# Expert weights through ten places instead of eight, gate/up weights in 32 KB rows

## The chip, the cores and the metric

One core of one Trainium2 chip runs the kernel. The metric is the device time of one execution in microseconds. All data is float32.

## What is computed

A decoder layer: a projection, two token mixers side by side, a merge and an output projection, and then a mixture of experts, which is most of the work. 256 tokens and 16 meta tokens go in, each of width 1024. What matters here is the last part:

```python
logits = (tokens @ w_router + b_router).astype(f32)
top_logits, top_idx = lax.top_k(logits, TOP_K)          # 4 of 32 experts
top_w = jax.nn.softmax(top_logits, axis=-1)
...
gu = xb @ w_gate_up[e] + b_gate_up[e]                    # 1024 -> 2048
gate = jnp.minimum(gu[:, ::2], SWIGLU_LIMIT)
up = jnp.clip(gu[:, 1::2], -SWIGLU_LIMIT, SWIGLU_LIMIT)
glu = gate * jax.nn.sigmoid(gate * SWIGLU_ALPHA)
return ((up + 1.0) * glu) @ w_down[e] + b_down[e]        # 1024 -> 1024
```

An expert has 8 MB of gate/up weights and 4 MB of down weights, 32 experts have 384 MB, and every expert is chosen by some token, so all of it is read from HBM once.

## The kernel before

The program is written by hand for each engine; semaphores order the engines. Up to about 260 us it computes the mixers, the merge and the output projection, then the router, then which tokens go to which expert (a chain of small instructions on DVE and PE). After that runs the loop over items. An item is one expert with up to 64 of its tokens; here there are 32 items.

**Pieces and places.** The weights of an item come in six pieces of 2 MB, 16 KB in each of 128 partitions: pieces 0 to 3 are gate/up, 4 and 5 are down. Counted through the whole loop, piece `r` lies in place `r % PLACES` of `ring`; there are eight places, and `HOME` says which stretch of `ring` a place is. `load_piece` (the DMA is issued at line 286) loads one, and the place has a semaphore `landed`. PE adds one to `piece_used` when its last matmul of a piece is done.

**The order of the loads.** All weight loads are issued by SP. Before the loop SP loads pieces 0 to 4 while the mixers end (it waits for `o_mm`, `og_used` and `br_mm` in turn, since the places held other tensors), then the router weights and the small bias rows, and pieces 5 to 7 when the output projection is done (`wo_mm`). From piece 8 on, `load_round` waits for `piece_used` to reach r - 7, that is, until the piece that held the place is consumed. The loop covers `ROUND` = 4 items, 24 pieces or three trips through the places.

**One item on PE** (`item`): four bias matmuls of 32 rows (`ohb` times `bgu`), then for each gate/up piece a wait for `landed` and eight matmuls (two records each in the trace), then `add_last` (the item before is added into x's sum in PSUM) and `gather` (the tokens of the next item), transposes of the activated hidden values and of the gathered tokens, and the two down pieces, eight matmuls each. DVE and ACT do the activation between them.

**The routing on DVE.** Just ahead of the loop DVE builds `oh`, a one-hot table of the experts of the items, and a second copy of it in partitions 32 to 63 (`oh_up`), from which `expert_of` makes the operand `ohb` of the bias matmuls. The bias rows `bgu` lie in 64 partitions, 2048 elements each.

Of the kernel before, what the change touches and what calls it, by code (L numbers as in the profile page):

```python
# [20 lines left out]
P = 128  # L21
META, SEQ = 16, 256
TOK = META + SEQ
D = 1024
# [10 lines left out]
EXTRA = 16  # L35
# [4 lines left out]
PLACES = 8  # L40
ROUND = 4
HOME = [2, 4, 5, 7, 3, 6, 0, 1]
# [41 lines left out]
def build(nc, a, out):  # L84
    with ExitStack() as ctx:
# [15 lines left out]
        grow = sb("grow", [4, 2 * P])  # L101
# [19 lines left out]
        ringf = ring[:, :, :].rearrange("p a b -> p (a b)")  # L121
# [74 lines left out]
        x2 = at(w_mix, 0, TT, D)  # L196
        sumT = at(w_mix, 2048, KD, SEQ)
        xgT = at(w_mix, 4096, 2, 2, 2, SLOTS)
        xgS = at(w_mix, 8576, 512)
        squares = at(w_mix, 2048, D)  # L200
        hT = at(w_mix, 4608, 4, 2, SLOTS)
        gt = at(w_mix, 5120, 512)
        sgm = at(w_mix, 5632, 512)
        up = at(w_mix, 6144, 512)
        ysl = at(w_mix, 6656, 512)
        ctr = at(w_mix, 7168, SEQ)
        pick = at(w_mix, 7424, TT, SLOTS)
        pickw = at(w_mix, 7552, TT, 2, SLOTS)
        ohb = w_mix[0:2 * E, 7808:7808 + SLOTS]
        wrt = at(w_mix, 9472, KD, E)  # L210
        brt = w_mix[:, 9728:9728 + E]
        lgq = at(w_mix, 9760, TT, P)

        gain1, gain2, gain_x = pcol[:, 0:8], pcol[:, 8:16], pcol[:, 32:40]

        gatesf = gates[:, :, :].rearrange("p a b -> p (a b)")
        bgu = gatesf[0:2 * E, 0:2 * D]
        fgain = gatesf[:, 3 * D:4 * D]
# [12 lines left out]
        oh_up = rout[E:2 * E, 480:480 + ITEMS + 2]  # L231
        oh_both = rout[0:2 * E, 480:480 + ITEMS + 2]
        ohc = rout[0:E, 530:530 + EXTRA]
        j3 = rout[0:E, 578:626]
        half = rout[0:1, 626:628]
# [3 lines left out]
        iwt = at(rout, 1256, TT, ITEMS + 2)  # L239
# [4 lines left out]
        for n in """consts xload0 xload1 meta rows ident_in gain1_in gain1_turned gain1_ready s5rows bload cload glu_w branch5_w branchh_w out_w expert_rows  # L244
# [4 lines left out]
                    proj proj_free bu bu_free ph rounded sines scanned xs5 ysum  # L249
                    gelu_in gelu_sig g5_ready glu_mm glu_sig f_sig q_sig og_sig f_ready logf  # L250
# [7 lines left out]
                    ct_mm ct_ready ysl_ready comb0 comb1 added0 added1 piece_used w_last xgs_ready xg_turned  # L258
# [8 lines left out]
        gu_d = a["w_gate_up"].rearrange("l e (i p j) n -> p (l e i) (j n)", i=UP, p=P)  # L267
# [14 lines left out]
        def load_piece(q, e, r):  # L282

            i, place = r % PIECES, r % PLACES
            src = gu_d[:, bass.ds(e * UP + i, 1), :] if i < UP else dn_d[:, bass.ds(e * DOWN + (i - UP), 1), :]
            q.dma_start(ring[:, HOME[place]:HOME[place] + 1, :], src).then_inc(landed[place], 16)

# [4 lines left out]
        def _(sp):  # L292
# [46 lines left out]
            more_rounds = sp.value_load(idx[0:1, ITEMS + 3:ITEMS + 4], min_val=E // ROUND - 1, max_val=ITEMS // ROUND - 1)  # L339

            def load_round(q, last):

                e = None
                for r in range(PLACES, ROUND * PIECES + (0 if last else PLACES)):
# [5 lines left out]
            with sp.Fori(0, more_rounds) as q:  # L350
                load_round(q, False)
            load_round(more_rounds, True)
# [7 lines left out]
        def _(pool):  # L360
# [6 lines left out]
            pool.dma_start(grow[:, :], a["norm2_gain"].rearrange("l (i c) -> (l i) c", c=2 * P)).then_inc(s["grow_in"], 16)  # L367
# [216 lines left out]
        def _(pe):  # L584
# [92 lines left out]
            for j in range(2):  # L677
                last = tr(ps[6][:, 32 + 4 * j:36 + 4 * j], grow[:, :].rearrange("p (c j) -> p j c", j=2)[:, j, :], 4)
# [203 lines left out]
            def turn_gathered(w, bank):  # L882

                pe.wait_ge(s["xgs_ready"], w + 1)
                for b in range(2):
                    for j in range(2):
                        part = xgS[:, 256 * b:256 * (b + 1)].rearrange("p (c j) -> p j c", j=2)[:, j, :]
                        last = tr(ps[bank][:, (2 * b + j) * P:(2 * b + j + 1) * P], part)
                last.then_inc(s["xg_turned"], 1)
# [31 lines left out]
            pe.wait_ge(s["expert_rows"], 32)  # L921
# [572 lines left out]
```

## Time and profile before

| what | value |
|---|---|
| median of 3 runs | 1208.69 us (1208.61 to 1208.96) |
| the profiled execution, its own time | 1208.81 us |
| its span, first to last instruction | 1207.0 us |
| PE busy | 1163.8 us (96% of the span) |
| DVE busy | 442.1 us (37%) |
| ACT busy | 181.5 us (15%) |
| read from HBM | 434.53 MB |
| weight loads gate/up, down | 128 and 64, of 2048 KB each |

The profiled execution's own time is 1.8 us more than its span (what lies around the instructions), and 0.12 us above the median. "PE busy" counts matmuls in flight; "PEld" is the load of the stationary operand into PE. A releaser behind an arrow is what ended a wait. In the time of the loop PE is busy nearly all the time by its records, and so are the DMA engines.

### The profile page before, as it was taken

To read this page: it belongs to the slowest core of one execution; us is meant where nothing else is said; L and a number is where in the kernel's file an instruction comes from. 1 tells how busy PE (TensorE), PEld (TensorE's weight loads), DVE (VectorE), ACT (ScalarE), POOL (GpSimd) and SP (SyncE) were. 2 spreads that over 40 slices of the span, in tenths; PEclk is the share of its full clock that TensorE was granted. 3 is DMA by queue.
4 is the path that set the end of the run, shared out by engine and by line. 5 is a ranking of instruction groups with operands and counts; after the bars stand their busy time and mean duration, and the time that the engine had idled before them with its cause. 6 is when DMAs were issued, how large, how long until landed. Compare 5 with 4: busy or idle time off the path is not lost.

```text
span 1207.0 us, 14299 instructions
## 1 busy us (share of the span) xinstructions
PE 1163.8 (96%) x5532; PEld 501.3 (42%) x5532; DVE 442.1 (37%) x1108; ACT 181.5 (15%) x330; POOL 3.6 (0%) x11
## 2 busy tenths in 40 slices
PE   8999999999999999999999999999999999999996
PEld 7757798763333333333333333333333333333332
DVE  6889883242322222222333222222222222222224
ACT  4435632020000000000000000000000000000002
POOL 1000000000000000000000000000000000000000
PEclk9999998998999999999999999999999999999999
DMA  6444304836999999999999999999999999999994
GB/s 214 175 173 179 137 1 189 342 153 282 426 430 426 429 430 427 428 431 427 428 429 428 428 428 429 427 430 428 428 430 428 427 430 428 428 430 428 428 429 179
DMA packets 47528, 435.91 MB, mean 361 GB/s; under 512 B 10044, under 2 KB 10240, under 8 KB 22864
## 3 DMA queue, kind: packets, MB, share of 16 engines
q1 hardware_dynamic: 46912, 434.93, 86.2%
q10 hardware_dynamic: 400, 0.58, 0.1%
q8 instruction: 15, 0.25, 0.1%
q0 software_dynamic: 192, 0.08, 0.0%
q14 instruction: 9, 0.07, 0.0%
HBM read 434.53 MB, written 1.05 MB: 361 GB/s over the span
## 4 chain that ended last, share of the span: by engine, by line
PE 68%; DMA 26%; DVE 3%; ACT 1%; issue 1%; ACTq 0%; SPq 0%; DVEq 0%
PE ps L586 65%; DMA ring<-in_w_gate_up 25%; PE ps L589 4%; DVE ring L989 1%; ACT ring L382 1%; DMA ring<-in_s_lambda_im 0%; ACT L382 0%; DVE ring L992 0%; DVE ring L1162 0%; DVE ring L995 0%; DVE w_mix L995 0%; DVE rout L992 0%; DVE rout L995 0%; ACT small L382 0%; DVE x L989 0%
## 5 line engine op out<-in xcount | busy, mean ns | idle before, releaser
L586 PE MATMUL ps<-ring,w_mix 128*64 128x512 f32 (+1 forms) x3168 | 710.2, 591 | 23.1 <-DMA ring<-in_w_gate_up 21.8
L586 PEld LDWEIGHTS ps<-ring,w_mix 128*64 128x64 f32 (+1 forms) x3168 | 227.6, 139 | 458.4 <-issue 399.8
L992 DVE TENSOR_SCALAR w_mix<-ps 128x256 f32<-128x256 f32 x128 | 45.3, 416 | 613.2 <-PE ps L586 613.2
L586 PE MATMUL ps<-ring 128*128 128x256 f32 (+7 forms) x920 | 195.7, 397 | 2.7 <-DVE ring L989 2.2
L586 PEld LDWEIGHTS ps<-ring 128*128 128x128 f32 (+2 forms) x920 | 144.0, 187 | 51.1 <-issue 30.0
L586 PE MATMUL ps<-w_mix 64*128 64x512 f32 (+3 forms) x624 | 142.5, 569 | 0.7 <-issue 0.7
L382 ACT ACTIVATE w_mix<-ps 128x512 f32<-128x512 f32 (+1 forms) x104 | 55.0, 529 | 396.3 <-PE ps L589 212.4
L382 ACT ACTIVATE w_mix<-w_mix 128x512 f32<-128x512 f32 x32 | 20.1, 630 | 514.7 <-DVE w_mix L992 514.7
L989 DVE TENSOR_TENSOR x<-ps,x 128x512 f32<-128x512 f32 x136 | 84.3, 679 | 18.1 <-PE ps L586 18.1
L586 PEld LDWEIGHTS ps<-w_mix 64*128 64x128 f32 (+3 forms) x624 | 51.7, 161 | 88.2 <-issue 86.3
L989 DVE TENSOR_TENSOR ring<-ring 128x256 f32<-128x256 f32 (+5 forms) x182 | 76.4, 472 | 6.6 <-PE ps L586 3.7
L589 PEld LDWEIGHTS ps<-cst,w_mix 128*128 128x128 f32 x328 | 43.1, 194 | 58.8 <-issue 26.0
L589 PE MATMUL ps<-cst,w_mix 128*128 128x128 f32 x328 | 63.4, 307 | 0.6
L992 DVE TENSOR_SCALAR w_mix<-cst,rout 128x64 f32<-128x64 f32 x194 | 44.5, 285 | 0.5 <-issue 0.5
L1447 DVE COPY w_mix<-ps 128x512 f32<-128x512 f32 x32 | 22.1, 691 | 50.8 <-PE ps L589 50.8
L586 PE MATMUL ps<-gates,w_mix 32*64 32x512 f32 x256 | 35.7, 627 | 0.6 <-DVE w_mix L989 0.6
L382 ACT ACTIVATE ring<-ring 128x272 f32<-128x272 f32 (+5 forms) x50 | 29.9, 602 | 9.6 <-DVE ring L989 6.6
L989 DVE TENSOR_TENSOR ring<-ps,ring 128x272 f32<-128x272 f32 x64 | 23.6, 427 | 4.0 <-PE ps L586 3.8
L989 DVE TENSOR_TENSOR w_mix<-ps,pcol 128x512 f32<-128x512 f32 x33 | 22.5, 682 | 0.2 <-PE ps L589 0.2
L989 DVE TENSOR_TENSOR w_mix<-w_mix 128x512 f32<-128x512 f32 x32 | 22.1, 692 | 1.1
L995 DVE SCALAR_TENSOR_TENSOR w_mix<-w_mix 128x512 f32<-128x512 f32 x32 | 22.1, 691 | 1.1
L382 ACT ACT_TABLE_LOAD x15 | 19.2, 1283 | 7.1 <-issue 3.6
(145 smaller groups left out, 241.7 us busy)
## 6 DMA issues: line engine op xcount, KB each, us to landing
ring<-in_w_gate_up SPq DMA_DIRECT2D x128, 2048.0 KB, 31.2
ring<-in_w_down SPq DMA_DIRECT2D x64, 2048.0 KB, 35.2
ring<-in_w_in SPq DMA_DIRECT2D x9, 2048.0 KB, 7.9
ring<-in_w_out SPq DMA_DIRECT2D x1, 4096.0 KB, 12.9
w_mix<-in_w_branch_s SPq DMA_DIRECT2D x1, 2048.0 KB, 13.6
w_mix<-in_w_branch_hgrn SPq DMA_DIRECT2D x1, 2048.0 KB, 12.6
x<-in_x SPq DMA_DIRECT2D x2, 512.0 KB, 4.4
w_mix<-in_s_w_glu SPq DMA_DIRECT2D x1, 1024.0 KB, 10.1
```

Of the source, the lines that this page charges most:

```text
L382: return nc.scalar.activation(o, i, fn, **k)
L586: return nc.tensor.matmul(o, l, r, start=start, stop=stop, skip_group_check=True)
L589: return nc.tensor.transpose(o, i, ident[0:n, 0:n])
L989: return V.tensor_tensor(out=o, in0=i0, in1=i1, op=op)
L992: return V.tensor_scalar(o, i, s1, s2, op0, op1) if op1 is not None else V.tensor_scalar(o, i, s1, None, op0)
L995: return V.scalar_tensor_tensor(out=o, in0=i0, scalar=sc, in1=i1, op0=op0, op1=op1)
L1447: V.tensor_copy(hT, ps[3][:, :].rearrange("p (a b c) -> p a b c", a=4, b=2)).then_inc(s["hT_ready"], 1)
```

## The change

It has three parts.

1. **Ten places.** `gates` and `w_mix` become one tensor `mixed` of 14336 elements per partition; when the mixers are done, its upper 8192 hold two more places (`home` gives a place's address). What lay there in the loop moves to the lower part of `mixed` and into a stretch of `cst` that is no longer needed. `bgu` is spread over 128 partitions of 512 elements: `oh_up` gets three copies instead of one, and the four bias matmuls use rows 0-31, 32-63, 64-95 and 96-127. The final gain `fgain` is loaded behind the last weights instead of ahead of the loop. The items before the loop (`HEAD` = 2) are written out, and the loop covers 5 items, 30 pieces, three trips through ten places; the number of items is padded to 2 + 5k, which for 32 is again 32.
2. **The loads ahead of the loop.** All of pieces 0 to 9 are loaded before the first `piece_used`; piece 7 goes where piece 3 went in the order, pieces 3 and 4 go where piece 4 went, piece 5 behind the bias rows, and 6, 8 and 9 behind `wo_mm`.
3. **Pairs.** Each partition of a 4 MB half of the gate/up weights now holds 32 KB that are contiguous in HBM. From piece 12 on, pieces 0 and 1 of an item, and 2 and 3, are loaded by one DMA of 4 MB (`load_pair`) into two places side by side. It waits until both places are free, and PE waits for it at the first of the two pieces. Down pieces are loaded singly, as before. Since `w_gate_up`'s rows are dealt out otherwise, the gathered tokens are transposed with another stride (`turn_gathered`, and `grow`, `gain_x` for the same order).

```diff
-PLACES = 8
-ROUND = 4
-HOME = [2, 4, 5, 7, 3, 6, 0, 1]
+PLACES = 10
+HEAD, ROUND = 2, 5
+HOME = [4, 5, 2, 3, 8, 9, 6, 7, 0, 1]
+RING = 8
...
+        def load_pair(q, e, r):
+
+            i, place = r % PIECES, r % PLACES
+            q.dma_start(home(place, 2).rearrange("p (a n) -> p a n", a=1), gu2_d[:, bass.ds(e * (UP // 2) + i // 2, 1), :])\
+                .then_inc(landed[place], 16)
+
+        def in_pair(r):
+            return r >= PLACES and r % PIECES < UP
...
-            for r in range(3):
+            for r in (0, 1, 2):
                 load_piece(sp, 0, r)
             sp.wait_ge(s["og_used"], 1)
-            load_piece(sp, 0, 3)
+            load_piece(sp, 1, 7)
             sp.wait_ge(s["inv_mm"], 1)
             sp.wait_ge(s["br_mm"], 8)
-            load_piece(sp, 0, 4)
+            for r in (3, 4):
+                load_piece(sp, 0, r)
...
-            sp.wait_ge(s["mrg_ready"], 4)
-            for g in range(2):
-                sp.dma_start(bgu[E * g:E * (g + 1), :], a["b_gate_up"].rearrange("l e n -> (l e) n")).then_inc(s["expert_rows"], 16)
-            sp.dma_start(fgain, a["final_norm_gain"].rearrange("(o n) -> o n", o=1).to_broadcast([P, D])).then_inc(s["lastgain"], 16)
...
+            load_piece(sp, 0, 5)
...
             sp.wait_ge(s["wo_mm"], 4)
-            for r in range(5, PLACES):
-                load_piece(sp, r // PIECES, r)
+            for r in (6, 8, 9):
+                load_piece(sp, 1, r)
...
-                    sp.wait_ge(s["piece_used"], q * (ROUND * PIECES) + (r - PLACES + 1))
-                    load_piece(sp, e, r)
...
+                    if not in_pair(r):
+                        sp.wait_ge(s["piece_used"], q * (ROUND * PIECES) + (r - PLACES + 1))
+                        load_piece(sp, e, r)
+                    elif r % 2 == 0:
+                        sp.wait_ge(s["piece_used"], q * (ROUND * PIECES) + (r - PLACES + 2))
+                        load_pair(sp, e, r)
...
                 def place(i):
                     r = m * PIECES + i
-                    pe.wait_ge(landed[r % PLACES], quad * (ROUND * PIECES // PLACES * 16) + 16 * (r // PLACES + 1))
-                    return ring[:, HOME[r % PLACES], :]
+                    if not (in_pair(r) and r % 2):
+                        first, more = landings(r)
+                        pe.wait_ge(landed[r % PLACES], 16 * first if q is None else q * (16 * more) + 16 * first)
+                    return home(r % PLACES)
...
-            V.tensor_copy(oh_up[:, 0:E], ident[E:2 * E, E:2 * E])
-            V.memset(oh_up[:, ITEMS:ITEMS + 2], 0.0)
+            for g in range(1, 4):
+                V.tensor_copy(oh_up[g - 1][:, 0:E], ident[E * g:E * (g + 1), E * g:E * (g + 1)])
+                V.memset(oh_up[g - 1][:, ITEMS:ITEMS + 2], 0.0)
```

SP's queue ahead of the loop, from the end of the mixers (`o_mm`) to the last load that waits for `wo_mm`. Before:

```order
L286 DMA ring<-in_w_gate_up 128x4096 [waits o_mm]
L286 DMA ring<-in_w_gate_up 128x4096 x2
L286 DMA ring<-in_w_gate_up 128x4096 [waits og_used]
L286 DMA ring<-in_w_down 128x4096 [waits br_mm,inv_mm]
L324 DMA w_mix<-in_w_router 128x8x32 [waits br_mm]
L325 DMA w_mix<-in_b_router 128x32
L329 DMA gates<-in_b_gate_up 32x2048 [waits mrg_ready]
L329 DMA gates<-in_b_gate_up 32x2048
L330 DMA gates<-in_final_norm_gain 128x1024
L333 DMA w_mix<-in_b_down 32x512 [waits ysl_ready]
L286 DMA ring<-in_w_down 128x4096 [waits wo_mm]
L286 DMA ring<-in_w_gate_up 128x4096 x2
```

and now:

```order
L295 DMA ring<-in_w_gate_up 128x4096 [waits o_mm]
L295 DMA ring<-in_w_gate_up 128x4096 x2
L295 DMA ring<-in_w_gate_up 128x4096 [waits og_used]
L295 DMA ring<-in_w_gate_up 128x4096 [waits br_mm,inv_mm]
L298 DMA mixed<-in_w_down 128x4096
L354 DMA mixed<-in_w_router 128x8x32 [waits br_mm]
L355 DMA mixed<-in_b_router 128x32
L358 DMA mixed<-in_b_gate_up 32x512 x4
L298 DMA mixed<-in_w_down 128x4096
L364 DMA mixed<-in_b_down 32x512 [waits ysl_ready]
L295 DMA ring<-in_w_gate_up 128x4096 [waits wo_mm]
L295 DMA ring<-in_w_gate_up 128x4096 x2
```

Seven pieces instead of five are now issued ahead of the wait for `wo_mm`, one of them directly ahead of the router weights.

SP's loop, one item of it (ISA rows are the waits on `piece_used`). Before:

```order
L286 ISA [waits piece_used]
L286 DMA ring<-in_w_down 128x4096
L347 REGISTER_ALU
L286 ISA [waits piece_used]
L286 DMA ring<-in_w_down 128x4096
L346 ISA
L346 TENSOR_LOAD idx
L346 ISA x2
L347 REGISTER_ALU
L286 ISA [waits piece_used]
L286 DMA ring<-in_w_gate_up 128x4096
L347 REGISTER_ALU
```

and now:

```order
L298 ISA [waits piece_used]
L298 DMA ring<-in_w_down 128x4096
L377 ISA
L377 TENSOR_LOAD idx
L377 ISA x2
L382 REGISTER_ALU
L304 ISA [waits piece_used]
L304 DMA ring<-in_w_gate_up 128x8192
L382 REGISTER_ALU
L304 ISA [waits piece_used]
L304 DMA mixed<-in_w_gate_up 128x8192
L379 REGISTER_ALU
```

An item has four loads now where it had six; the two of gate/up weights have 8192 elements per partition.

DVE in the routing, from the copies of the one-hot table to the operands of the last matmuls. Before:

```order
L1374 COPY rout<-cst 32x32
L1375 COPY rout<-cst 32x32
L1376 MEMSET rout 32x2
L1377 CAST idx<-cst 1x32
```

and now:

```order
L1411 COPY rout<-cst 32x32
L1413 COPY rout<-cst 32x32
L1414 MEMSET rout 32x2
L1413 COPY rout<-cst 32x32
L1414 MEMSET rout 32x2
L1413 COPY rout<-cst 32x32
L1414 MEMSET rout 32x2
L1415 CAST idx<-cst 1x32
```

Two copies and two memsets come in here; a little further on a copy of 32x16 (L1395) becomes three of 32x20 (L1433), and one of three small writes of `idx` goes.

## Rows read from the trace of the kernel before

**Rows 1.** The page: bytes moved in 40 equal slices of the span (GB/s)
```profile
GB/s 214 175 173 179 137 1 189 342 153 282 426 430 426 429 430 427 428 431 427 428 429 428 428 428 429 427 430 428 428 430 428 427 430 428 428 430 428 428 429 179
```
**Rows 2.** Windows: start:end and length, busy by engine, PEclk, DMA share, GB/s
```profile
400.00:600.00 200.00, 199.57 (x938) 67.08 (x936) 54.59 (x134) 15.46 (x28) 0.00 (x0) 1.00 1.01 428
700.00:1100.00 400.00, 381.88 (x1769) 124.64 (x1766) 104.43 (x254) 29.93 (x54) 0.00 (x0) 1.00 1.01 429
```
**Rows 3.** The chain that ended last, in time: start, length, what
```profile
609.16 22.27 PE ps L586 x104
...
636.92 22.27 PE ps L586 x104
...
676.48 33.24 DMA ring<-in_w_gate_up
709.76 7.44 PE ps L586 x32
...
734.50 33.95 DMA ring<-in_w_gate_up
...
1145.60 33.96 DMA ring<-in_w_gate_up
1179.60 7.44 PE ps L586 x32
```
**Rows 4.** Timeline of PE, last two items: start, length, what, [idle before <-releaser]
```profile
1150.24 3.65 PE L586 MATMUL ps<-ring,w_mix 128*64 128x512 f32 x16 [1.24 <-DMA ring<-in_w_gate_up]
...
1166.76 1.09 PE L586 MATMUL ps<-gates,w_mix 32*64 32x512 f32 x8
1167.77 10.58 PE L586 MATMUL ps<-ring,w_mix 128*64 128x512 f32 x48
1179.60 3.65 PE L586 MATMUL ps<-ring,w_mix 128*64 128x512 f32 x16 [1.25 <-DMA ring<-in_w_gate_up]
1183.19 3.85 PE L586 MATMUL ps<-w_mix 64*128 64x512 f32 x16
```
**Rows 5.** Windows around the start of the loop (columns as in rows 2)
```profile
270.00:274.00 4.00, 2.73 (x19) 1.24 (x16) 3.12 (x22) 0.60 (x1) 0.00 (x0) 1.00 1.00 430
278.00:284.00 6.00, 6.00 (x22) 1.81 (x20) 0.00 (x0) 0.00 (x0) 0.00 (x0) 0.62 0.00 0
284.00:286.00 2.00, 2.00 (x13) 0.56 (x9) 0.00 (x0) 0.00 (x0) 0.00 (x0) 1.00 0.70 131
286.00:288.00 2.00, 2.00 (x12) 0.70 (x10) 0.00 (x0) 0.00 (x0) 0.00 (x0) 1.00 0.73 287
```
**Rows 6.** Timeline of SP, loads of the places that come free first
```profile
284.24 3.74 SPq L286 DMA_DIRECT2D ring<-in_w_gate_up  x2
294.51 0.33 SPq L286 DMA_DIRECT2D ring<-in_w_down  x1
307.40 0.34 SPq L286 DMA_DIRECT2D ring<-in_w_gate_up  x1
312.37 0.33 SPq L286 DMA_DIRECT2D ring<-in_w_gate_up  x1
```
**Rows 7.** Timeline of DVE in the routing
```profile
269.95 0.17 DVE L1375 COPY rout<-cst 32x32 f32<-32x32 f32 x1
270.07 0.06 DVE L1376 MEMSET rout<- 32x2 f32 x1
270.14 0.17 DVE L1377 CAST idx<-cst 1x32 int32<-1x32 f32 x1
```
**Rows 8.** Windows in which all the data moved in rows of 2 KB, 2 KB, 4 KB, 4 KB
```profile
70.00:73.00 3.00, 3.00 (x8) 1.33 (x7) 3.00 (x9) 0.00 (x0) 0.00 (x0) 1.00 1.05 404
89.00:92.00 3.00, 3.00 (x12) 1.66 (x11) 2.77 (x8) 2.11 (x6) 0.00 (x0) 1.00 1.05 409
76.00:79.00 3.00, 3.00 (x8) 1.33 (x7) 0.00 (x0) 2.60 (x6) 0.00 (x0) 1.00 1.03 412
94.00:97.00 3.00, 3.00 (x29) 1.60 (x28) 3.00 (x8) 1.39 (x4) 0.00 (x0) 1.00 1.02 408
```
**Rows 9.** The loads of line 286, from issue to landing
```profile
DMA to landing us min/median/max: 7.7/31.3/35.3
```
**Rows 10.** Timeline about the router weights: SP, then DVE and PE
```profile
230.72 0.38 SPq L324 DMA_DIRECT2D w_mix<-in_w_router  x1
...
236.27 0.42 DVE L989 TENSOR_TENSOR w_mix<-w_mix,pcol 128x256 f32<-128x256 f32 x1 [3.24 <-DMA w_mix<-in_w_router]
...
244.26 0.60 PE L589 MATMUL ps<-cst,x 128*128 128x128 f32 x4
```

More of the change, by code:

```diff
@@ L230, in build @@
         oh = rout[0:E, 480:480 + ITEMS + 2]
[L231 to L235, printed above, removed]
+        oh_up = [rout[E * g:E * (g + 1), 480:480 + ITEMS + 2] for g in range(1, 4)]
+        oh_all = rout[:, 480:480 + ITEMS + 2]
+        ohc = rout[0:E, 534:534 + EXTRA]
+        j3 = rout[0:E, 576:576 + 3 * EXTRA]
+        half = rout[0:1, 636:638]
         slT = rout[0:E, 640:640 + SEQ]
@@ L257, in build @@
                     pick_ready gathered xg_ready gate_in gate_sg h_done
[L258 removed]
+                    ct_mm ct_ready ysl_ready comb0 comb1 added1 piece_used w_last xgs_ready xg_turned
                     grow_in down_bias last_sum
@@ L284, in load_piece, with landings @@
             i, place = r % PIECES, r % PLACES
-            src = gu_d[:, bass.ds(e * UP + i, 1), :] if i < UP else dn_d[:, bass.ds(e * DOWN + (i - UP), 1), :]
-            q.dma_start(ring[:, HOME[place]:HOME[place] + 1, :], src).then_inc(landed[place], 16)
+            if i < UP:
+                q.dma_start(home(place).rearrange("p (a n) -> p a n", a=1), gu_d[:, bass.ds(e * (UP // 2) + i // 2, 1), i % 2, :])\
+                    .then_inc(landed[place], 16)
+            else:
+                q.dma_start(home(place).rearrange("p (a n) -> p a n", a=1), dn_d[:, bass.ds(e * DOWN + (i - UP), 1), :])\
+                    .then_inc(landed[place], 16)
+        def load_pair(q, e, r):
+            i, place = r % PIECES, r % PLACES
+            q.dma_start(home(place, 2).rearrange("p (a n) -> p a n", a=1), gu2_d[:, bass.ds(e * (UP // 2) + i // 2, 1), :])\
+                .then_inc(landed[place], 16)
+        def in_pair(r):
+            return r >= PLACES and r % PIECES < UP
+        def landings(r):
+            alone = [n for n in range(r % PLACES, r + 1, PLACES) if not (in_pair(n) and n % 2)]
+            per_round = [n for n in range(PLACES, PLACES + ROUND * PIECES)
+                         if n % PLACES == r % PLACES and not (in_pair(n) and n % 2)]
+            return len(alone), len(per_round)
         block = ctx.enter_context(nc.Block())
@@ L676, in _ @@
             tr(ps[6][:, 8:32], prow[:, :], 24)
-            for j in range(2):
-                last = tr(ps[6][:, 32 + 4 * j:36 + 4 * j], grow[:, :].rearrange("p (c j) -> p j c", j=2)[:, j, :], 4)
+            for j in range(4):
+                last = tr(ps[6][:, 32 + 2 * j:34 + 2 * j], grow[:, :].rearrange("p (c j) -> p j c", j=4)[:, j, :], 2)
             last.then_inc(s["rows_turned"], 1)
@@ L884, in turn_gathered @@
                 pe.wait_ge(s["xgs_ready"], w + 1)
[L885 to L888, printed above, removed]
+                for j in range(4):
+                    last = tr(ps[bank][:, j * P:(j + 1) * P], xgS.rearrange("p (c j) -> p j c", j=4)[:, j, :])
                 last.then_inc(s["xg_turned"], 1)
@@ L938, in item @@
                 for b in range(2):
-                    rows = slice(E * b, E * (b + 1))
                     for h in range(2):
-                        last = mm(ps[b][SLOTS * h:SLOTS * (h + 1), :], ohb[rows, :],
-                                  bgu[rows, D * h + 512 * b:D * h + 512 * b + 512], True, False)
+                        rows = slice(E * (2 * b + h), E * (2 * b + h + 1))
+                        last = mm(ps[b][SLOTS * h:SLOTS * (h + 1), :], ohb[rows, :], bgu[rows, :], True, False)
                 last.then_inc(s["ohb_used"], 1)
@@ L968, in item @@
                     if i == 0:
-                        turn_last(pe.snap(w + 2))
-            with pe.Fori(0, n_rounds) as quad:
-                for m in range(ROUND):
-                    item(quad, m)
-            add_last(n_rounds * ROUND)
+                        turn_last(on(w + 2))
+            for m in range(HEAD):
+                item(m)
+            with pe.Fori(0, n_rounds) as q:
+                for m in range(HEAD, HEAD + ROUND):
+                    item(m, q)
+            add_last(n_rounds * ROUND + HEAD)
         @block.vector
@@ L1383, in _ @@
             V.tensor_copy(first, ps[2][0:E, 1:2])
[L1384 removed]
+            link(ts(half[:, 0:1], ps[2][0:1, 2:3], 1.0 / ROUND, 0.4, MU, AD))
             link(ts(half[:, 0:1], half[:, 0:1], MAGIC, None, AD))
             link(ts(half[:, 0:1], half[:, 0:1], MAGIC, None, SU))
[L1387 to L1388 removed]
+            ts(idx[0:1, ITEMS + 2:ITEMS + 3], half[:, 0:1], float((E - HEAD) // ROUND), None, AD)
             ts(idx[0:1, ITEMS:ITEMS + 1], half[:, 0:1], float(ROUND), float(E), MU, AD).then_inc(s["count_ready"], 1)
[L1390 removed]
+            js, ja, jb = (j3[:, EXTRA * k:EXTRA * (k + 1)] for k in range(3))
             link(ts(js, iota_e[0:E, 0:EXTRA], first, None, SU))
@@ L1394, in _ @@
             link(tt(oh[:, E:ITEMS], ja, jb, MU))
-            V.tensor_copy(oh_up[:, E:ITEMS], oh[:, E:ITEMS])
+            for g in range(1, 4):
+                V.tensor_copy(oh_up[g - 1][:, E:ITEMS], oh[:, E:ITEMS])
             link(ts(js, js, 1.0, None, AD))
```

110 lines of the change are left out of this document (59 added, 51 removed).

## The prediction, made before the changed kernel ran

> **What bounds the kernel now.** I began with the page's row of bytes moved [rows 1]. From slice 11 of 40 to the last but one it stands at 426 to 431 GB/s and never gives way, whatever PE is doing: the loop streams weights at one rate. The windows confirm it: 428 and 429 GB/s with a DMA share of 1.01 over 200 and 400 us [rows 2]. Next the chain of waits [rows 3]. Up to about 676 us one item follows another on PE in 27.76 us (609.16 to 636.92) and the chain never leaves PE. From 676 us on it goes in hops of two items through a weight load, the wait of PE ending at 709.76, then 16 items later at 1179.60: 29.37 us per item, 4.894 us per piece of 2 MB, which is 2.097 MB at 428.5 GB/s. So PE would need 27.76 us for an item and DMA needs 29.37. PE lives off the pieces loaded ahead for some 14 items and waits for weights in each item after that. The end of the kernel is therefore **the end of the weight stream, plus what PE does after it**; PE's 96% is no bound by itself, and time saved on PE inside the loop is worth nothing.
>
> Where PE waits: 48 records after the bias matmuls, three pieces of 16, so at piece 3 of an item [rows 4]. The last such wait ends at 1179.60, and what follows (piece 3, `add_last`, both down pieces, the last sum, the norm, the store) is the tail, which nothing shortens.
>
> The other end of the stream: eight pieces are there when the loop begins, and nothing moves between 278 and 284 us [rows 5]; then the first consumed place is loaded, issued at 284.24 [rows 6]. Counting bytes from the right edge of the window that ends at 288, (131 + 287) x 2 = 836 KB or 1.95 us of data: the data begins 2.0 us after the issue. From there 182 pieces (8 to 189) go past until the wait at 1179.60 ends; 182 x 4.894 = 890.7, and the rest, 4.7 us, is start, landing and small gaps.
>
> **The change, term by term.**
>
> *Two pieces more before the stream, -9.8.* Ten instead of eight are loaded before the first `piece_used`, in time when the engines idle. The stream to the last wait is 180 pieces instead of 182: 2 x 4.894. The pieces that move forward need cover. Piece 4 now goes out directly behind piece 3 and ahead of the router weights, and delays them by 4.9 us. They landed at 236.23 and DVE waited for them; with 4.9 more, 0.42 for the product with the gain and 0.69 for the first addition to `x` it is 242.3, and PE wants that addition at 244.26 [rows 10]. Covered, with 2.0 us to spare; without this cover each us would be one on the path. The bias rows and piece 5 land some 5 to 10 us later than the rows they replace did and are not wanted before the loop, 30 us later. `fgain` is issued behind the last weights in a queue that is then full; it lands some 3 us after them and is wanted after the last sum, over 10 us later. Nothing.
>
> *The routing, +0.6.* DVE gets two copies and two memsets of `oh_up`. A copy and its memset take 0.19 us of its time (269.95 to 270.14) [rows 7], so 0.38; two more narrow copies are bounded by 0 and 0.17 each, I take 0.15; one write of `idx`, some 0.09, goes. This chain leads to the first item, so the first consumed piece is 0.6 us later, and the stream with it.
>
> *Gaps in the young stream, +3.6.* Until the places run short, a load is issued when PE has consumed enough, and PE has a rhythm: the fourth piece is consumed at 294.51, the sixth at 307.40, the seventh some 0.4 before 312.37 [rows 6]. Before, each load waits for one piece and the queue stays just filled. Now pieces 12 and 13 wait for the fourth, 14 and 15 for the sixth. With 0.6 for the routing and 2.0 from issue to data: pieces 10 and 11 run from 286.8 to 296.6; the first pair begins at 297.1 (gap 0.5) and ends at 306.9; the second begins at 310.0 (gap 3.1) and ends at 319.8. Pieces 16 and on are issued well before that, and since PE gains 1.6 us on the stream with each item no later pair finds the queue empty. In the steady state at most three places hold pieces not yet consumed, so seven are on order, 34 us of data; the loads of before stand 31.3 us in the queue [rows 9].
>
> *Rows of 32 KB, -4.4.* 60 pairs replace 120 loads. Each engine moves 8 rows a load, so 480 rows per engine go away. The price of a row isn't shown at this size. Rates by row length: 404 and 409 GB/s at 2 KB, 412 and 408 at 4 KB [rows 8], 428.5 at 16 KB. A 2 MB load at 406, 410 and 428.5 takes 5.165, 5.115 and 4.894 us, and has 64, 32 and 8 rows per engine: (5.165 - 4.894) / 56 = 4.8 ns a row, (5.115 - 4.894) / 24 = 9.2 ns. By the one 480 rows are 2.3 us, by the other 4.4. The step from 4 to 16 KB is nearest to the one made here, and I take 4.4. The lower bound is no gain at all, or a loss (below).
>
> The Trainium skill (DMA: Bandwidth & Descriptors, Why small descriptors are slow) gives a fixed overhead of about 3 cycles per packet, at the fabric clock that it names an estimate of 3.5 ns, 1.7 us for 480 rows. By that the sum would be -3.7 us. The trace shows more for a row than this: 4.8 and 9.2 ns.
>
> *The tail, +3.6.* PE now waits for the pair ahead of piece 2, while the bytes of piece 3 arrive when they did. After the last wait PE has one gate/up piece more to do: 3.59 us (1179.60 to 1183.19) [rows 4]. The two down pieces land 10 us later and are wanted later still.
>
> *At nothing:* the bias matmuls keep their number and size, and four row groups take the place of two; if they ran one after the other it would cost an item 1 us at most [rows 4], and 27.76 + 1 is still below 29.2 us. The other stride of the transposes, the registers of the loop and the new addresses are PE, DVE and SP time inside the loop, under the same cover.
>
> Sum: -9.8 + 0.6 + 3.6 - 4.4 + 3.6 = **-6.4 us**. The profiled execution took 1208.81 us, 0.12 above the median; from the median it is 1202.3. The cover is thinner afterwards: an item of the stream takes 29.2 us, PE's 27.76.
>
> **Rivals.**
>
> *The long rows bring nothing* (the engines still move 16 KB at a time, or the cost goes by bytes). For it: between 2 and 4 KB the rate hardly rises [rows 8]. Against: it does rise to 16 KB. Then the sum is -2.0: 1206.7, within the noise.
>
> *The long rows read more slowly.* No row of before is longer than 16 KB; in a pair each engine walks 32 KB at one stretch and the engines start twice as far apart in HBM. The mechanism would sit in the 60 pair loads alone, visible as a lower GB/s in steady windows. Its bound is the rate at 4 KB rows, 410: 120 x 0.221 = 26.5 us, so 1233. It turns the sign from 2.0 + 2.4 = 4.4 us on, spread over 587 us of pairs: 0.75%, a rate of the pairs below 425. Against: the rate rose with every step in row length so far. At 1.5% it is 1206.7 + 8.8 = 1215.5.
>
> *The stream gets fast enough for PE's pace.* If each load carried a fixed price of its own, halving the gate/up loads would give much. Then PE's own rhythm is the end: the fourth piece of item 0 is consumed at 294.51, that of item 31, 31 x 27.76 later, at 1155.1, where it was 1183.2. With 0.6 for the routing that is 27.5 us less, 1181.2. The Trainium skill (SBUF — State Buffer, The DMA setup-cost knee) has such a rule: a fixed 2 us per transfer, so join them; 60 fewer transfers would be 120 us. Against it stands that a 2 MB load takes 4.894 us, less than bytes at 428.5 GB/s plus anything fixed: queued loads overlap. A half-way case is likelier: rows worth twice my price and no gap at the second pair, 1202.3 - 4.4 - 3.6, some 1195 to 1198.
>
> **How the numbers follow.** Forecast with its own spread (row price 2.3 to 4.4, gaps 2 to 5 us, 1200 to 1205.5): 0.60. Long rows bring nothing: 0.15. Slower rows: 0.13, mostly 1209 to 1220. Still faster: 0.12, nearly all above 1195. The range 1197 to 1208 holds the forecast, the case without a gain and half of the faster one. A measurement of this kernel tells 0.2% (2.4 us) from no change: faster is 0.60 + 0.12, same is the 0.15, slower 0.13.
>
> **What would show it.** GB/s in the steady windows at 430 to 431 with an item of 29.2 us; at 428 the rows bring nothing, below 427 they cost. 60 gate/up loads of 4096 KB and 62 single ones behind the ten first. An idle stretch of the engines between 306 and 310 us. PE's waits ahead of piece 2, and 31 us from the end of the last wait to the end of the span, where it was 27.4. The prediction is wrong if PE never waits for weights, if the stream has later gaps, or if the first item starts more than 1 us later.

## The result, and the profile after

The changed kernel takes **1202.76 us** (median of five runs, 1201.16 to 1204.25), beside 1208.69 us for the kernel before (1208.34 to 1210.34 in the same rounds). The ratio is 0.9949, 95% interval 0.9934 to 0.9963: 5.9 us less. The profiled execution has a span of 1200.9 us, where it was 1207.0. The forecast was 1202.3.

The page's row of bytes moved, after (it answers to [rows 1]):

```profile
GB/s 215 175 167 185 140 1 172 405 208 256 391 434 427 429 433 428 429 433 430 429 433 430 429 433 430 429 433 430 429 433 429 430 433 426 432 429 429 431 431 141
```

From slice 12 on the level is 426 to 434, a step above the 426 to 431 of before. The slice ahead of it, with 391, is the gap that the prediction described. The windows show both (columns as in [rows 2]); the first three answer to [rows 5], the last two to [rows 2]:

```profile
278.00:284.00 6.00, 6.00 (x22) 1.55 (x16) 0.00 (x0) 0.00 (x0) 0.00 (x0) 0.54 0.00 0
284.00:286.00 2.00, 2.00 (x12) 0.57 (x10) 0.00 (x0) 0.00 (x0) 0.00 (x0) 1.00 0.00 0
286.00:288.00 2.00, 2.00 (x12) 0.70 (x10) 0.00 (x0) 0.00 (x0) 0.00 (x0) 1.00 0.96 254
305.00:308.00 3.00, 3.00 (x20) 0.76 (x16) 0.00 (x0) 0.00 (x0) 0.00 (x0) 1.00 0.59 251
308.00:310.00 2.00, 2.00 (x16) 0.62 (x16) 0.00 (x0) 0.60 (x1) 0.00 (x0) 1.00 0.91 262
310.00:312.00 2.00, 2.00 (x12) 0.62 (x10) 0.00 (x0) 0.00 (x0) 0.00 (x0) 1.00 0.69 279
400.00:600.00 200.00, 199.69 (x938) 67.22 (x936) 54.62 (x133) 15.45 (x28) 0.00 (x0) 1.00 1.01 431
700.00:1100.00 400.00, 385.28 (x1794) 128.04 (x1792) 109.24 (x266) 30.31 (x55) 0.00 (x0) 1.00 1.00 431
```

SP's timeline after, the loads of the places that come free first (it answers to [rows 6]):

```profile
285.10 3.76 SPq L298 DMA_DIRECT2D ring<-in_w_down  x2
295.38 0.34 SPq L304 DMA_DIRECT2D ring<-in_w_gate_up  x1
308.24 0.33 SPq L304 DMA_DIRECT2D mixed<-in_w_gate_up  x1
312.83 3.79 SPq L298 DMA_DIRECT2D ring<-in_w_down  x2
```

Pieces 10 and 11 at 285.10, the first pair at 295.38, the second only at 308.24. The chain that ended last (it answers to [rows 3]) leaves PE after 16 items and then goes through a weight load every second item:

```profile
724.76 36.22 DMA mixed<-in_w_gate_up
761.02 10.87 PE ps L623 x48
...
1111.60 10.87 PE ps L623 x48
1131.73 38.25 DMA ring<-in_w_gate_up
1170.03 10.87 PE ps L623 x48
```

14 items lie between 761.02 and 1170.03: 29.215 us an item, 4.869 a piece, where it was 4.894. PE's timeline in the last item (it answers to [rows 4]):

```profile
1160.70 1.09 PE L623 MATMUL ps<-mixed,cst 32*64 32x512 f32 x8
1161.72 7.09 PE L623 MATMUL ps<-ring,mixed 128*64 128x512 f32 x32
1170.03 7.09 PE L623 MATMUL ps<-ring,mixed 128*64 128x512 f32 x32 [1.22 <-DMA ring<-in_w_gate_up]
1177.04 3.85 PE L623 MATMUL ps<-mixed,cst 64*128 64x512 f32 x16
```

PE waits after 32 records, at piece 2, and has 32 ahead of it instead of 16. From 1170.03 to the end of the span it is 30.9 us, where it was 27.4. And the page's DMA issues (KB each, median us to landing):

```profile
ring<-in_w_gate_up SPq DMA_DIRECT2D x48, 4096.0 KB, 37.7
ring<-in_w_down SPq DMA_DIRECT2D x50, 2048.0 KB, 35.8
mixed<-in_w_gate_up SPq DMA_DIRECT2D x12, 4096.0 KB, 35.6
mixed<-in_w_down SPq DMA_DIRECT2D x14, 2048.0 KB, 34.3
...
ring<-in_w_gate_up SPq DMA_DIRECT2D x8, 2048.0 KB, 17.1
```

60 gate/up loads of 4 MB; of 64 down loads two are ahead of the loop.

Both kernels, and every experiment, can be cut at the same two points: the first load of the loop, and the end of PE's last wait for weights.

| kernel | first load | to the last wait's end | from there to the end of the span | first load to end |
|---|---|---|---|---|
| before | 284.24 | 895.36 | 27.4 | 922.8 |
| after | 285.10 | 884.93 | 30.9 | 915.8 |
| after, profiled again (experiment 12) | 284.42 | 884.13 | 30.9 | 915.0 |
| after, with idle matmuls ahead of the loop (experiment 8) | 283.28 | 885.37 | 30.9 | 916.2 |

The last three rows issue the same loads from the first one on, so they show how far such a cut scatters by itself: 1.2 us. One profile against another tells differences above that, and no smaller ones.

### The profile page after: what moved, and what is told of

Read it like the earlier page. It is cut to its first block, busy times and chain, and to the rows that moved or that the text cites. A ratio compares the mean times of both kernels' runs of the same rounds, so it can differ in the third digit from the quotient of the medians.

```text
span 1200.9 us, 14064 instructions
## 1 busy us (share of the span) xinstructions
PE 1162.0 (97%) x5534; PEld 503.8 (42%) x5534; DVE 442.9 (37%) x1112; ACT 181.5 (15%) x330; POOL 3.6 (0%) x11
## 4 chain that ended last, share of the span: by engine, by line
PE 68%; DMA 26%; DVE 3%; ACT 1%; issue 1%; ACTq 0%; SPq 0%; DVEq 0%
PE ps L623 64%; DMA ring<-in_w_gate_up 19%; DMA mixed<-in_w_gate_up 6%; PE ps L626 4%; DVE ring L1028 1%; ACT ring L419 1%; DMA ring<-in_s_lambda_im 0%; ACT L419 0%; DVE ring L1031 0%; DVE ring L1199 0%; DVE ring L1034 0%; DVE mixed L1034 0%; DVE rout L1031 0%; DVE rout L1034 0%; ACT mixed L419 0%
## 5 line engine op out<-in xcount | busy, mean ns | idle before, releaser
L623 PE MATMUL ps<-ring,mixed 128*64 128x512 f32 (+1 forms) x2560 | 572.5, 590 | 15.7 <-DMA ring<-in_w_gate_up 14.8
L623 PEld LDWEIGHTS ps<-ring,mixed 128*64 128x64 f32 (+1 forms) x2560 | 187.8, 139 | 362.9 <-issue 330.9
L1031 DVE TENSOR_SCALAR mixed<-ps 128x256 f32<-128x256 f32 x128 | 45.4, 418 | 606.0 <-PE ps L623 606.0
L623 PE MATMUL ps<-mixed,cst 64*128 64x512 f32 (+2 forms) x784 | 163.0, 616 | 1.3 <-issue 0.7
L623 PE MATMUL ps<-mixed 128*64 128x512 f32 (+2 forms) x704 | 151.3, 562 | 3.0 <-DMA mixed<-in_w_gate_up 2.9
L623 PEld LDWEIGHTS ps<-mixed,cst 64*128 64x128 f32 (+2 forms) x784 | 45.5, 151 | 112.1 <-issue 111.3
L623 PEld LDWEIGHTS ps<-mixed 128*64 128x64 f32 (+2 forms) x704 | 54.5, 140 | 88.7 <-issue 79.9
L419 ACT ACTIVATE mixed<-ps 128x512 f32<-128x512 f32 (+1 forms) x87 | 48.4, 557 | 276.3 <-PE ps L623 223.9
L626 PE MATMUL ps<-cst,mixed 128*128 128x128 f32 x262 | 49.4, 310 | 0.6
L1031 DVE TENSOR_SCALAR cst<-cst,rout 128x64 f32<-128x64 f32 x194 | 44.8, 288 | 0.5 <-issue 0.5
```

What stands on the lines that cost most here:

```text
L419: return nc.scalar.activation(o, i, fn, **k)
L623: return nc.tensor.matmul(o, l, r, start=start, stop=stop, skip_group_check=True)
L626: return nc.tensor.transpose(o, i, ident[0:n, 0:n])
L1031: return V.tensor_scalar(o, i, s1, s2, op0, op1) if op1 is not None else V.tensor_scalar(o, i, s1, None, op0)
```

## The experiments

The prediction came true as a sum of terms of both signs. Such a sum can be right by terms that are wrong together, so each was taken apart. Unless said otherwise an edit is one of the changed kernel; times are medians, and ratios are to the kernel before, timed on the same chip in the same rounds (1208.71, 1208.98 and 1208.67 us in the three sets of four). The changed kernel itself was timed again in the third set only (experiment 12).

### 1. No pairs

```diff
         def in_pair(r):
-            return r >= PLACES and r % PIECES < UP
+            return False
```

> Ten places, but every gate/up load single, 2 MB in rows of 16 KB. The sum: 120 loads regain their 480 longer rows per engine (+4.5), the gaps of the young stream close (-3.9) and the last wait is at piece 3 again (-3.4): 1200.0, so faster than the changed kernel. Item of the stream 29.4 us, last wait to end 27.4 us, GB/s 428. Rival, the pairs are what gained and the gaps and the tail cost nothing: 1207 or more.

Measured: **1200.09 us** (1197.75 to 1201.4), 0.9933 [0.9920, 0.9947]. The profile is of the fastest of its runs; the cut takes out what of that lies ahead of the first load. First load to the last wait's end 885.14 us, to the end of the span 912.6: 3.2 less than with pairs. Steady windows:

```profile
400.00:600.00 200.00, 199.69 (x938) 67.32 (x936) 55.73 (x137) 15.77 (x29) 0.00 (x0) 1.00 1.01 428
700.00:1100.00 400.00, 389.39 (x1814) 128.55 (x1812) 109.25 (x266) 30.91 (x56) 0.00 (x0) 1.00 1.01 428
```

The rate is back at 428 and the gap and the long tail (27.4 us) are gone. So the third part of the change, taken alone, costs some 3 us; what it gains by the rate (4.5) is less than what it gives back at the start (3.9) and at the end (3.5).

### 2. Only pieces 0 and 1 in pairs

```diff
-            return r >= PLACES and r % PIECES < UP
+            return r >= PLACES and r % PIECES < 2
```

> Only pieces 0 and 1 of an item go as a pair, 2 and 3 singly. The sum: half of the rows' gain is kept (+2.25), the gap ahead of the second pair, 3.1 to 3.4 us, closes, the tail is 27.4 us again (-3.4): 1198.2, faster than both kernels. Rival, gaps and tail cost nothing: 1205.

Measured: **1199.06 us** (1197.58 to 1199.46), 0.9924 [0.9911, 0.9937]; first load to end 912.7 us. The time is within 1 us of what was expected, but not by the way expected. PE's timeline in its last item:

```profile
1155.45 1.09 PE L623 MATMUL ps<-mixed,cst 32*64 32x512 f32 x8
1158.00 12.24 PE L623 MATMUL ps<-ring,mixed 128*64 128x512 f32 x56 [1.46 <-DMA ring<-in_w_gate_up]
```

The wait has moved to piece 0. The pair of pieces 0 and 1 holds back piece 0 by one piece's time, and PE's slack in an item, 29.2 - 27.76 = 1.4 us, doesn't cover that; after it PE isn't held at piece 3 any more. The tail is 37.8 us in place of 27.4. Against no pairs at all it is even in the profile (912.7 and 912.6).

### 3. 4 MB loads with the old rows of 16 KB

Rows dealt out as before the change, two pieces still loaded by one DMA:

```diff
-            q.dma_start(home(place, 2).rearrange("p (a n) -> p a n", a=1), gu2_d[:, bass.ds(e * (UP // 2) + i // 2, 1), :])\
+            q.dma_start(home(place, 2).rearrange("p (a n) -> p a n", a=2), gu_d[:, bass.ds(e * UP + i, 2), :])\
```

> Pairs of 4 MB as in the change, same waits, but each partition gets two rows of 16 KB from two places of HBM (the dealing of before). The sum (length of rows counts): gaps and tail stay, the rows' gain goes, 1206.8 with 428 GB/s in the steady windows, item 29.3 us. Rival (number of transfers counts): as the changed kernel, 1202.8, 431 GB/s.

Measured: **1205.83 us** (1202.76 to 1206.48), 0.9974 [0.9965, 0.9984]; first load to the last wait's end 888.50, 3.6 us more than after, and the rate:

```profile
400.00:600.00 200.00, 199.65 (x938) 67.16 (x936) 54.63 (x133) 15.45 (x28) 0.00 (x0) 1.00 1.01 428
700.00:1100.00 400.00, 382.37 (x1780) 126.92 (x1778) 107.13 (x261) 29.91 (x54) 0.00 (x0) 1.00 1.01 428
```

It is the length of the row that raises the rate, not the number of transfers (the rival, at 1202.8 us and 431 GB/s): with half as many gate/up loads and the old rows it stands where it stood. 3.57 us over 480 rows is 7.4 ns a row, and 6.5 to 9.1 ns against the three profiles of the changed kernel's stream.

### 4. Pieces 8 and 9 only when the loop has begun

```diff
-            for r in (6, 8, 9):
+            load_piece(sp, 1, 6)
+            sp.wait_ge(s["piece_used"], 1)
+            for r in (8, 9):
                 load_piece(sp, 1, r)
```

> The changed kernel, with the loads of pieces 8 and 9 held back until the first piece is consumed, so that eight pieces are there at the start of the stream. The sum: two pieces more go through the stream (+9.7), but they fill the engines while the pairs wait for their places (-3.9): 1208.6. Rival (the ten places help by a deeper queue, not by the early start): 1202.8. Rival (gaps are no cost of the pairs): 1212.5.

Measured: **1207.43 us** (1206.12 to 1209.13), 0.9989 [0.9981, 0.9998]; first load of the loop (now piece 8) to the last wait's end 890.36, to the end 921.3: 5.5 us more than after. Two pieces are 9.7 us, and what the stream needs beyond its pieces falls from 8.5 us to 890.36 - 182 x 4.869 = 4.2: the gap closes, since the stream has two more pieces to bring when the pairs wait. Both rivals lie outside the range of the runs: that the ten places help by a deeper queue and not by the early start (1202.8), and that the pairs cost no gap (1212.5). The time is 1.2 us below the expected 1208.6; 0.9 of that is a first load at 284.21 instead of 285.10.

### 5. The same loads with rows of 8 KB

The two gate/up halves of an item are 4 MB loads of four rows of 8 KB per partition. The rows of `w_gate_up` in the pairs are dealt to the partitions otherwise than the tokens are turned, so this kernel's products are not the reference's.

```diff
-            q.dma_start(home(place, 2).rearrange("p (a n) -> p a n", a=1), gu2_d[:, bass.ds(e * (UP // 2) + i // 2, 1), :])\
+            q.dma_start(home(place, 2).rearrange("p (u n) -> p u n", u=4), gu8_d[:, bass.ds(e * (UP // 2) + i // 2, 1), :, :].rearrange("p a u n -> p (a u) n"))\
```

> The changed kernel with each 4 MB pair read in rows of 8 KB, four per partition (the rows of w_gate_up are dealt out otherwise, so what is computed is not the reference's). 1440 rows more per engine. If a row costs the 9.4 ns that the two steady rates (4.894 and 4.869 us a piece) give: +13.5, 1216.3. Rival, a row costs 4.8 ns as between 2 and 4 KB: +6.9, 1209.7. If row length only acts above 16 KB: 1206.

Measured: **1214.09 us** (1213.46 to 1214.93), 1.0040 [1.0026, 1.0055]; first load to the last wait's end 897.46, 12.5 us more than after for 1440 more rows per engine, 8.7 ns a row, where 9.4 was expected (1216.3 us).

```profile
400.00:600.00 200.00, 199.69 (x938) 67.15 (x936) 54.71 (x134) 15.45 (x28) 0.00 (x0) 1.00 1.01 424
700.00:1100.00 400.00, 376.04 (x1750) 124.26 (x1748) 101.52 (x248) 28.70 (x52) 0.00 (x0) 1.00 1.01 424
```

424, 428, 431 GB/s at 8, 16 and 32 KB, with the down rows at 16 KB in all three.

### 6. Pieces 12 to 15 singly, everything later in pairs

SP's first round is written out, with four pieces loaded by `load_piece`; PE waits for each of them.

```diff
-            with sp.Fori(0, rounds) as q:
+            load_more(0, PLACES, PLACES + ROUND * PIECES, early=EARLY)
+            with sp.Fori(1, rounds) as q:
```

> The changed kernel with its first two pairs (pieces 12 to 15) loaded singly; all later pairs stay. If the gaps are made by these two pairs alone: -3.9 and +0.1 for the shorter rows: 1199.0, engines busy from 296 us on. Rival, the queue has gaps for another reason (later pairs, the start of the loop): 1202.8.

Measured: **1199.61 us** (1198.6 to 1201.23), 0.9922 [0.9909, 0.9935]. The cut is less kind: first load to the last wait's end 883.76, only 1.2 us less than after, where the gap was 3.9. That is within the scatter of the cut; what is sure is that most of the 3.9 didn't come back. The gap had moved one item on:

```profile
330.00:336.00 6.00, 6.00 (x32) 1.78 (x33) 0.50 (x4) 0.98 (x2) 0.00 (x0) 1.00 0.94 358
336.00:342.00 6.00, 6.00 (x30) 2.01 (x28) 0.00 (x0) 0.00 (x0) 0.00 (x0) 1.00 0.94 399
342.00:348.00 6.00, 6.00 (x30) 2.01 (x28) 0.00 (x0) 0.00 (x0) 0.00 (x0) 1.00 0.95 407
```

In the changed kernel 330 to 360 us stands at 430. Against that level some 1.8 us of data are missing here. The likely reason: an idle stretch early in the stream gives PE a lead over it, and that lead is what covers the next pairs; close the first gap and the next pair meets a queue that is nearly empty. The other part of the gain in time came from the first load, 283.13 instead of 285.10, which has another cause (experiment 8).

### 7. The same, and pieces 2 and 3 singly in the last round

```diff
+            load_more(but_last, PLACES, PLACES + ROUND * PIECES, late=True)
```

> As e6, and in the last five items pieces 2 and 3 are loaded singly, so that the last waits are not for a pair at piece 2. Tail -3.4, but PE then waits for the pair of pieces 0 and 1 at piece 0, as in the run with that pair alone, +1.0; rows +0.4: 1197.1. Rival, the tail's 3.4 us is hidden by the down pieces: as e6.

Measured: **1199.88 us** (1198.45 to 1201.62), 0.9926 [0.9913, 0.9939]; first load to end 913.5, 1.1 less than experiment 6, where 1197.1 us had been expected. The 3.5 us of the tail didn't come back. PE's timeline two items ahead of the end, and the windows there:

```profile
1126.63 1.09 PE L630 MATMUL ps<-mixed,cst 32*64 32x512 f32 x8
1130.72 15.65 PE L630 MATMUL ps<-ring,mixed 128*64 128x512 f32 x64 [3.00 <-DMA ring<-in_w_gate_up]
```

```profile
1131.00:1135.00 4.00, 4.00 (x12) 1.09 (x10) 0.00 (x0) 0.00 (x0) 0.00 (x0) 0.58 1.01 430
1136.00:1140.00 4.00, 4.00 (x22) 1.34 (x20) 0.00 (x0) 0.00 (x0) 0.00 (x0) 1.00 1.01 430
```

With pieces 2 and 3 single, the pair of pieces 0 and 1 holds PE as in experiment 2, here for 3.0 us at piece 0; the granted clock then fell to a mean of 0.58 for 4 us, so 64 records took 15.65 us where the next item's took 13.95. After that PE runs to the end without a wait.

### 8. Ten idle matmuls ahead of the loop

`keep_warm` is the kernel's own helper: matmuls of `ones` by `ones`, 128x128, into a bank that nobody reads.

```diff
             gather(0, 3)
+            keep_warm(8)
...
             pe.wait_ge(s["count_ready"], 1)
+            keep_warm(2)
```

> The changed kernel with ten matmuls of ones in the two waits of PE ahead of the loop (272 to 274 and 276.7 to 277.2 us). In all profiles so far PE's granted clock is halved for 3.4 or 6.8 us around 276 to 283, where the first piece is consumed, and the stream starts with it. If the thin work ahead of the loop brings the low clock: full clock through item 0, stream 1.7 to 3.4 us earlier: 1199.4 to 1201, with less spread from run to run. Rival, the low clock comes anyway: 1202.8.

Measured: **1200.02 us** (1196.86 to 1201.38), 0.9918 [0.9907, 0.9930]. In the routing PE waits for DVE again and again. After such a stretch the changed kernel's PE starts the first item at a mean granted clock of 0.54 (278 to 284 us, above), the kernel before at 0.62 [rows 5]; such a mean is part the lower level, 0.50 or 1.2 GHz, and part the upper, 1.00 or 2.4 GHz. With the ten matmuls:

```profile
278.00:284.00 6.00, 5.88 (x33) 1.94 (x33) 0.77 (x3) 0.26 (x1) 0.00 (x0) 1.00 0.00 0
```

33 records in those 6 us, where it was 22. The stream's first load is issued when PE has consumed the first piece, and the end of a kernel that DMA bounds moves with it. The time of that load depends on two things: when item 0 starts, and at which clock it runs. PE's first bias matmul of item 0 in the kernel before, the changed one and this one:

```profile
276.35 1.98 PE L586 MATMUL ps<-gates,w_mix 32*64 32x512 f32 x8 [0.56 <-DVE w_mix L989]
277.17 1.98 PE L623 MATMUL ps<-mixed,cst 32*64 32x512 f32 x8 [0.57 <-DVE mixed L1028]
278.41 1.09 PE L623 MATMUL ps<-mixed,cst 32*64 32x512 f32 x8
```

| profiles | mean granted clock, 278 to 284 us | item 0 starts | from there to the first load |
|---|---|---|---|
| before | 0.62 | 276.35 | 7.89 |
| after | 0.54 | 277.17 | 7.93 |
| after again (12) | 0.80 | 278.74 | 5.68 |
| experiments 1 to 7 | 0.54 to 0.91 | 277.24 to 278.69 | 5.5 to 7.9 |
| with the idle matmuls (8, 9, 10, 11) | 1.00 | 278.41, 277.09, 278.75, 278.36 | 4.87, 4.86, 4.87, 4.90 |

So the full clock is worth 0.6 to 3.1 us here, by how long the clock was low. The start of item 0 differs by as much as 1.7 us from profile to profile of the changed kernel and its variants; what shifts it wasn't followed up. The median is 2.7 us lower than the changed kernel's first one; the ranges touch (the changed kernel's runs begin at 1201.16), but the intervals of the two ratios (0.9907 to 0.9930, and 0.9934 to 0.9963) don't. The sign is sure, the size isn't.

### 9. Pairs in the middle rounds only, and the idle matmuls

First and last round of loads single, four rounds (20 items, 40 pairs) as in the change, and the edit of experiment 8.

```diff
+            load_more(0, PLACES, PLACES + ROUND * PIECES, single=True)
+            with sp.Fori(1, but_last) as q:
...
+            load_more(but_last, PLACES, PLACES + ROUND * PIECES, single=True)
```

> Ten places, the warm matmuls of e8, and pairs only in the four middle rounds: the first round (pieces 12 to 39) and the last are loaded singly. The gap that closing the first one had moved to item 3 should be gone, the last waits are at piece 3 and the tail is 27.4 us. From the first load of the loop to the end of the span: 915.8 (changed kernel) - 3.9 - 3.4 + 0.8 for 10 pairs less = 909.4, first load at 282.1: 1193.3. Rival, the pairs' longer rows are the only thing of worth and the rest gives back what it gains: 1198 to 1200.

Measured: **1196.29 us** (1196.18 to 1196.64), 0.9902 [0.9889, 0.9915]: the fastest of all, 6.0 us below the changed kernel in the same rounds (experiment 12) and 12.4 below the one before. It is 3 us above what was expected; 0.7 of that is a slip in the expectation, which took 10 pairs less where it is 20.

### 10. No pairs, and the idle matmuls

> All loads single and the warm matmuls. First load of the loop at 282.1 plus 912.6 as in the run of singles: 1196.5. If the pairs in the middle are worth their place, 3 us above the kernel with pairs in the middle rounds; if not, equal.

Edit: those of experiments 1 and 8 together. Measured: **1196.98 us** (1196.71 to 1198.4), 0.9908 [0.9895, 0.9921]. Only 0.7 us above experiment 9, and 0.6 in the cut (912.4 and 913.0 from first load to end): forty pairs without a gap and without a longer tail bring some 0.6 us, where 3.0 were expected (40 x 8 rows x 9.4 ns). The runs of the two don't overlap (the slowest of experiment 9 took 1196.64), so there is a gain, but the cut alone wouldn't show it. The pairs did raise the rate, 430 and 431 GB/s against 428 and 429 in the windows from 500 to 900 us. The last section says what is known of where it went.

### 11. The kernel before, and the idle matmuls

The edit of experiment 8 in the kernel before.

> The kernel before with the warm matmuls alone. The first load of the loop, at 284.24 with a halved clock from 275.7 to 282.5, comes at 281.2 to 282.5: 1205.8 to 1207. Rival, the clock at the start of the loop has no part in the end of the stream: 1208.7.

Measured: **1207.51 us** (1206.11 to 1208.36), 0.9989 [0.9981, 0.9998]; first load 283.26, 1.0 earlier. The time is 0.5 us above the expected 1205.8 to 1207. The matmuls work in the kernel before too and are worth 1.2 us there: of what experiments 9 and 10 gain, most is the change's own (the two places).

### 12. The changed kernel again

> The changed kernel again, beside the others on the same chip: 1202.8, and a spread of runs of 2 to 3 us, which would follow from a low clock of 3.4 or 6.8 us at the start of the loop.

Measured: **1202.25 us** (1201.27 to 1204.06), 0.9954 [0.9941, 0.9968]. The spread of 2.8 us is the kernel's own, as in its first runs (3.1 us), while experiment 9 spreads over 0.5 us.

## Why the prediction was right

The forecast missed the median by 0.5 us, and its terms hold one by one within 0.3 us. That the total came within 0.5 is in part luck: the runs of the changed kernel spread over 3.1 us, and the start of the loop, which moves the first load by over 1 us from one profile to the next (experiment 8), was no part of the working. One reason given in it doesn't hold, and one reading is off: [rows 5] shows 131 GB/s already between 284 and 286 us, so the data begins less than 2.0 us after the issue, and more slowly than was counted. That start stands in both kernels and changes no term.

**What bounds the kernel.** Right. PE still waits for weights (12 and 3 waits in the whole trace, 17.7 us together), the stream never stops after 312 us, and every experiment moved the time by what it did to the stream, its start or the tail.

**Two places, -9.8.** Right. Experiment 4 gives them back: +5.4 us to the last wait, which is 9.7 less the 4.3 of the gap that closes. The cover for the earlier loads held, a little thinner than worked out: DVE takes up the router weights at 241.86 instead of 236.27, and its addition ends at 242.88, 1.5 us ahead of PE's matmul at 244.34.

**Routing, +0.6.** The first load is issued at 285.10 instead of 284.24, 0.86 later. The low clock isn't the cause of that: from item 0's start to the first load it is 7.89 us before and 7.93 after, and item 0 starts 0.82 later (276.35 and 277.17, experiment 8). The size fits. But the other profiles of the changed kernel and its variants start item 0 anywhere from 277.09 to 278.75, and the kernel before with idle matmuls at 278.36, so a few tenths between two profiles prove little, and this term isn't settled. Left out of the working was the clock itself, although the 0.62 stood in [rows 5]; it moves the first load by up to 3 us.

**Gaps, +3.6.** Right in place and size. The prediction had the engines idle from 306.9 us until the second pair's data at 310.0; the windows at 305 to 312 us show 251 to 279 GB/s, and the pair was issued at 308.24. What the stream needs beyond its pieces was 895.36 - 182 x 4.894 = 4.7 us and is 884.93 - 180 x 4.869 = 8.5: +3.9 before rounding, and +3.1 to +4.3 by all three profiles of the stream.

**No later pair finds the queue empty.** True of the changed kernel, and for a reason that was not given: the first gap itself made the lead. Experiment 6 took the gap away, the stream slowed one item later, and 1.2 of 3.9 us came back. A term of a sum isn't always what is to be had by removing it.

**Rows, -4.4.** Right: 180 x (4.894 - 4.869) = -4.5. The price per row, 9.2 ns by the step from 4 to 16 KB rows, measures 7.4 ns (experiment 3) and 8.7 ns (experiment 5) over the whole stream. The Trainium skill (DMA: Bandwidth & Descriptors, Why small descriptors are slow) gives a fixed overhead of about 3 cycles a packet, by its fabric clock an estimate of 3.5 ns. That is too low here by a factor of two to three.

**Tail, +3.6.** 30.9 - 27.4 = +3.5, at piece 2 as said.

**The sum.** -9.79 + 0.86 + 3.86 - 4.50 + 3.50 = -6.07, the difference of the two spans.

**The rivals.** Slower rows: refuted by the rate (431). Rows without an effect: the same. PE's pace and a fixed price per transfer: an item of the stream takes 29.215 us with two pairs and two single down pieces, so with 4.894 for each of the single ones a 4 MB load of 32 KB rows takes 9.71 us, 0.07 less than two of 2 MB, and experiment 3 shows that this comes from the rows. The Trainium skill (SBUF — State Buffer, The DMA setup-cost knee) puts a fixed 2 us on every transfer; this doesn't show between loads that are queued.

**What the prediction didn't ask** is whether the third part should be there. Its own terms, +3.6 - 4.4 + 3.6, say +2.8; experiment 1 measured +2.7 in time and 3.2 in the cut.

## What to carry to other kernels

Where a stream of loads sets the end, count what the DMA engines move before the first buffer comes free: two pieces more there were worth 9.8 us, all the rest of this change together cost 3.7. A larger load is also a larger thing to wait for: it needs two free places at once and releases its reader one piece later, so its gain in rate must be set against the first gap and the last piece, each of which is paid once; and a gap that is closed can turn up at the next large load. And whatever is late by a fixed amount when the stream starts, a slow clock on the engine that frees the first buffer for instance, is late at the end.

## What was not expected of the hardware

**A row costs a DMA engine about 13 ns.** The trace holds every packet of the 16 DMA engines. In the steady loop a packet of 8 KB takes 314 ns, one of 16 KB 615 ns, and one of 32 KB 1217 ns (means of 3258, 2614 and 868 packets between 500 and 600 us in experiment 5, experiment 1 and the changed kernel): 16 KB more are 602 ns, which leaves 13 ns that don't go by bytes. Of these 7.4 to 9.4 ns reached the stream (experiments 3 and 5, and the two steady rates). Packets of 16 KB were in the trace of before as well; a second size in the loop would have been needed to read the price there.

**The engines finish apart, and code travels with the weights.** In experiment 9 the 40 pairs should have brought 3.0 us over experiment 10. Strung end to end into 16 engines (the records name none), the packets of the weight stream end like this, counted from the first load: in experiment 10 the first engine after 892.5 us and the last after 894.8, in experiment 9 the first after 889.4 and the last after 894.2. The earliest end came 3.1 us sooner, the latest only 0.6, and the mean of the 16 ends 2.0; a piece is there only when the slowest engine has brought its rows. In its last two items, singles again, experiment 9 took 1166.91 - 1107.23 = 59.7 us against 58.7 in experiment 10.

Loads of two sizes aren't enough to explain it: the changed kernel's engines end 2.9 us apart in one profile and 2.0 in the other (experiment 12), those of experiment 1 2.0. There is a rival. Experiment 9 has two rounds of items written out, and its longer program is itself fetched by DMA while the weights stream. The pages' rows of the instruction queue (packets, MB, share), experiment 9 and experiment 10:

```profile
q8 instruction: 28, 0.46, 0.2%
q8 instruction: 18, 0.29, 0.1%
```

Ten blocks of 16 KB more, each of which took one engine 1.06 us: 10.6 us of one engine, 0.7 on the mean of 16. Behind the first load 17 such blocks came in experiment 9, five of them between 1046 and 1157 us; in experiment 10 there were 7, the last at 461 us. Experiment 7, which has its last round written out too, fetched five from 1058 us on, and its engines end 4.6 us apart. That fits, but which engine brought a block can't be read, and no run has pairs in the middle without the longer program. The cause stays open.

**The clock ahead of a stream.** Ten matmuls of 128x128 that compute nothing brought the granted clock of the first item to 1.00 in all four profiles that have them, where ten without them show 0.54 to 0.91. At the full clock the first load follows 4.9 us behind the start of item 0, otherwise 5.5 to 7.9 us. The time of the first load itself overlaps: 281.95 to 283.62 with them (experiments 8 to 11), 283.10 to 285.17 without. The spread shrank in experiments 9 and 10 (0.5 and 1.7 us, against 3.1), though not in experiment 8 (4.5), so that the warm start makes the time steadier isn't shown.
